# Expert stage of a one-core decoder block: 96 tokens by indirect row transfers, 160 tokens by dense plain float32 products

## What is computed

```python
q = (hf @ wq).reshape(T, PEER_HEADS, 2, PEER_DQ // 2)
s = jnp.einsum('thcd,hckd->thck', q, subkeys)
v_top, i_top = lax.top_k(s, PEER_TOPK)
...
ids = jnp.take_along_axis(cand_i, best_pos, axis=-1)
g = jax.nn.softmax(best_s, axis=-1)
...
ub = jnp.take(u_tab, idb, axis=0)
act = jax.nn.gelu(jnp.einsum('tkd,td->tk', ub, xb))
vb = jnp.take(v_tab, idb, axis=0)
return jnp.einsum('tk,tkd->td', (gb * act), vb)
```

## Time and profile before

| | |
|---|---|
| median of 3 runs | 2117.13 us (2108.36 to 2119.05) |
| the profiled execution's own time | 2113.12 us |
| its span in the profile | 2111.3 us |
| PE busy | 2066.6 us (98%) |
| DVE busy | 1383.3 us (66%) |
| ACT busy | 743.5 us (35%) |
| moved by DMA | 500.33 MB, 237 GB/s over the span |
| granted clock of PE | 0.993 of full speed in the mean |

### The profile page before, as it was taken

One profiled execution on the slowest core, in us unless ns is written; L12 is line 12 of the kernel. 1 busy time (PEld: TensorE's weight loads), 2 busy tenths in 40 slices (PEclk: granted clock), 3 DMA queues, 4 the chain that ended last, 5 costly groups with the idle time before them and its releaser, 6 DMA issues.

```text
span 2111.3 us, 30984 instructions
## 1 busy us (share of the span) xinstructions
PE 2066.6 (98%) x12256; PEld 1859.3 (88%) x12256; DVE 1383.3 (66%) x1840; ACT 743.5 (35%) x791; POOL 16.1 (1%) x30
## 2 busy tenths in 40 slices
PE   8999999989999999999999999999999999999998
PEld 6888888779988998999999999999999999999786
DVE  6685774968698976555555556556555555555797
ACT  2014114354212335343443443433433433433333
POOL 0000000000000000000000000000000000000100
PEclk9999999999999999999999999999999999999999
DMA  9999885864442666654655555555555546545995
GB/s 390 421 418 393 283 350 223 314 261 170 170 143 97 239 257 261 216 204 173 225 195 180 217 194 192 206 194 203 201 187 211 203 176 219 203 173 204 349 413 148
DMA packets 99208, 500.33 MB, mean 237 GB/s; under 512 B 8416, under 2 KB 41488, under 8 KB 42960
## 3 DMA queue, kind: packets, MB, share of 16 engines
q1 hardware_dynamic: 81840, 362.27, 46.5%
q10 hardware_dynamic: 13680, 112.20, 14.2%
q0 software_dynamic: 3632, 25.06, 3.0%
HBM read 477.32 MB, written 22.18 MB: 237 GB/s over the span
## 4 chain that ended last, share of the span: by engine, by line
PE 88%; DMA 7%; DVE 3%; ACT 1%; SPq 0%; issue 0%; ACTq 0%; DVEq 0%
PE ps L506 16%; PE ps L497 11%; PE ps L496 11%; PE ps L495 11%; PE ps L789 5%; DMA mod_first<-wmod 5%; PE ps L800 5%; PE ps L801 5%; PE ps L802 5%; PE ps L790 5%; PE ps L791 5%; PE ps L746 3%; PE ps L645 1%; DMA vraw<-vtab 1%; PE ps L646 1%; PE ps L647 1%
## 5 line engine op out<-in xcount | busy, mean ns | idle before, releaser
L497 PE MATMUL ps<-h_hi,wlo 128*128 128x256 f32 x1952 | 552.4, 283 | 0.0
L495 PE MATMUL ps<-h_hi,whi 128*128 128x256 f32 x1728 | 488.9, 283 | 1.6 <-DVE wlo L1533 1.6
L496 PE MATMUL ps<-h_lo,whi 128*128 128x256 f32 x1728 | 489.0, 283 | 0.0
L1571 DVE TENSOR_TENSOR yacc<-yacc,ps 128x512 f32<-128x512 f32 x208 | 142.9, 688 | 367.0 <-PE ps L802 367.0
L497 PEld LDWEIGHTS ps<-h_hi,wlo 128*128 128x128 f32 x1952 | 374.4, 192 | 0.0
L1537 DVE TENSOR_TENSOR vlo<-vraw,vhi 128x2048 fp32r<-128x2048 f32 x116 | 260.8, 2288 | 127.4 <-ACT vhi L1123 127.4
L495 PEld LDWEIGHTS ps<-h_hi,whi 128*128 128x128 f32 x1728 | 331.5, 192 | 3.8 <-DVE wlo L1533 1.8
L496 PEld LDWEIGHTS ps<-h_lo,whi 128*128 128x128 f32 x1728 | 331.5, 192 | 2.0
L1099 ACT ACTIVATE whi<-wraw 128x2048 fp32r<-128x2048 f32 x120 | 229.3, 1915 | 149.6 <-DMA wraw<-wst 144.2
L1533 DVE TENSOR_TENSOR wlo<-wraw,whi 128x2048 fp32r<-128x2048 f32 x120 | 269.5, 2285 | 16.4 <-ACT whi L1099 16.3
L1077 ACT ACTIVATE act_u<-ps 128x256 f32 (+1 forms) x128 | 49.1, 384 | 632.8 <-PE ps L497 569.9
(11 more groups left out here) (269 smaller groups left out, 2667.6 us busy)
## 6 DMA issues: line engine op xcount, KB each, us to landing
vraw<-vtab SPq DMA_DIRECT2D x116, 1024.0 KB, 6.8
wraw<-wst SPq DMA_DIRECT2D x111, 1024.0 KB, 4.9
wraw<-wst ACTq DMA_DIRECT2D x91, 1024.0 KB, 6.7
mod_ring<-wmod SPq DMA_DIRECT2D x58, 1024.0 KB, 10.9
mod_first<-wmod SPq DMA_DIRECT2D x22, 1024.0 KB, 20.0
gates_dram<-gstage ACTq DMA_DIRECT2D x4, 4096.0 KB, 17.0
gring<-gates_dram SPq DMA_DIRECT2D x64, 256.0 KB, 5.1
g_ring<-wmod POOLq DMA_DIRECT2D x16, 1024.0 KB, 9.2
```

The source lines that it names most:

```text
L495: mm(dst, hi, src_hi, start=first, stop=False)
L496: mm(dst, hi, src_lo, start=False, stop=False)
L497: return mm(dst, lo, src_hi, start=False, stop=last)
```

## The change

Tokens 0 to 95 (`N1`) get their picked rows, the other 160 (`N0`) stay dense.

*The 96 tokens.* DVE makes row numbers (`gidx`) of the first half's picks, PE turns h back to token rows (`hrow`). For each of the 128 picks GpSimd issues an indirect transfer that brings one row of `utab` for each of 96 tokens into a partition of its own (`gat`, 768 KB), and DVE multiplies and sums it with `hrow` (`dot`). After GeLU and gate (`row_weights`), 128 more transfers bring rows of `vtab`, and DVE adds each, times its weight, to `yacc` (`add_row`). There are two buffers `gat` for the first 30 dots and three after that.

*The 160 tokens.* U blocks and V blocks are plain products; nothing is rounded. The gates go straight from PSUM to `p0` in SBUF, with no way through DRAM, and are multiplied there in batches of 8 blocks (`weights`). V starts when all U blocks are done. The tile of V is the stationary operand and the 160 weights move, so y comes out turned; 6 banks of PSUM hold it over all 128 blocks. V is read in its stored order: `vnat[:, m, :]` takes for each partition a row of 8 KB, 1 MB after that of the partition before. `y_rows` turns y back with the last gain on the diagonal (`diag_g2`). The tiles of that gain are loaded from ACT's queue, each summed after six `add_row`.

The core of the diff:

```diff
-G2_RING = 3
-GB = 2
+G2_RING = 2
+N1 = 96
+N0 = T - N1
+PICKS = PEER_H * TOPK
 EARLY = 20
-LAG = 24
+HELD = 48
+BATCH = 8
+V_RING = 8
+LAST_V = 4
...
+            with sp.Fori(0, (NB - W_RING) // W_RING) as i:
+                for j in range(W_RING):
+                    n = N_U + W_RING + j
+                    sp.wait_ge(s_wmm, i * W_RING + (n - W_RING + 1))
+                    load_w(n % W_RING, i * W_RING + n)
+
+            for m in range(NB):
+                if m < W_RING:
+                    sp.wait_ge(s_wmm, N_U + NB - W_RING + m + 1)
+                elif m < V_RING:
+                    sp.wait_ge(s_p0, NB // BATCH)
+                else:
+                    sp.wait_ge(s_vmm, m - V_RING + 1)
+                sp.dma_start(v_slot(m), vnat[:, m, :]).then_inc(s_v[m % V_RING], 16)
...
+            def u_chunk(j, n, i, k):
+                chunk(j, n, i, k, src=h32, low=N1)
...
+            def v_tile(m, kk):
+
+                return mm(ps_y[kk], v_slot(m)[:, kk * P:(kk + 1) * P], p0[:, m, :], start=(m == 0 and kk % 3 == 0),
+                          stop=(m == NB - 1), skip_group_check=True)
...
+            def dot(k):
+
+                slot, count, _ = gather_slot(k)
+                if k == 0:
+                    dve.wait_ge(s_hrow, 4)
+                dve.wait_ge(s_gat[slot], count)
+                V.scalar_tensor_tensor(gat[slot][0:N1], gat[slot][0:N1], 1.0, hrow[0:N1], ALU.mult, ALU.mult,
+                                       accum_out=dots[0:N1, k:k + 1]).then_inc(s_used, 1)
...
+            for k in range(PICKS):
+                add_row(k)
+                if k % 6 == 5 and k // 6 < KD:
+                    add_g2(k // 6)
+                if k == 6 * KD:
                     part_done(5, M_G2)
-
+                    dve.wait_ge(s_modv, 4)
+                    dve.wait_ge(s_vmm, p0_free(141.5))
+                    V.tensor_tensor(diag_g2[:], ident.unsqueeze(1).to_broadcast([P, KD, P]),
+                                    modv[:, 5, :].unsqueeze(2).to_broadcast([P, KD, P]), ALU.mult).then_inc(s_dg2, 1)
+                    V.memset(ysb[:, :, 0:N1], 0.0).then_inc(s_yzero, 1)
...
+            pool.wait_ge(s_wmm, N_U)
+            pool.wait_ge(s_gidx, 1)
+            for g in range(2 * PICKS):
+                slot, _, held = gather_slot(g)
+                if g == S0_DOTS + 2:
+                    pool.wait_ge(s_gmm, SPREADS)
+                elif held is not None:
+                    pool.wait_ge(s_used, held + 1)
+                k = g % PICKS
+                pool.indirect_dma_start(out=gat[slot][0:N1], out_offset=None, in_=utab if g < PICKS else vtab,
+                                        in_offset=bass.IndirectOffsetOnAxis(ap=gidx[0:N1, k:k + 1], axis=0)).then_inc(s_gat[slot], 16)
```

More of the change, by code:

```diff
@@ L747, in spread @@
                 r.then_inc(s_gmm, 1)
[L749 to L750 removed]
+            for b in range(EARLY, HELD):
+                lo, hi = spreads_of(b)
                 def between(kk):
[L752 to L756 removed]
@@ L1090, in _ @@
                     act.wait_ge(s_gx, tt + 1)
                     A(pick_t[:, tt, 2], pick_t[:, tt, 2], ACT.Exp).then_inc(s_ge, 1)
-            for tt in range(TT):
-                act.wait_ge(s_pkt, tt + 1)
-                A(picks[:, :, tt * P:(tt + 1) * P], ps_spread[tt][:, 0:3], ACT.Copy).then_inc(s_pkr, 1)
-            def w_hi(j, n, i, k):
-                act.wait_ge(s_w[j], turns(i, k, W_RING) * 16)
-                A(whi[:, j], wraw[:, j], ACT.Copy).then_inc(s_whi, 1)
-            per = SPREADS // (EARLY - FIRST)
@@ new lines, in weights @@
+            def weights(i):
+                dve.wait_ge(s_wev, N_U + (i + 1) * BATCH)
+                blocks, held = slice(i * BATCH, (i + 1) * BATCH), i * BATCH % HELD
+                V.tensor_tensor(p0[:, blocks, :], act_u[:, held:held + BATCH, :], p0[:, blocks, :], ALU.mult).then_inc(s_p0, 1)
+            done = 0
+            for n in range(SPREADS):
+                one_hots(n)
+                while done < (n + 1) * S0_DOTS // SPREADS:
+                    dot(done)
+                    done += 1
@@ new lines, in _ @@
+            dve.wait_ge(s_gev, SPREADS)
+            for i in range(NB // BATCH):
+                if i < HELD // BATCH:
+                    until = S0_DOTS + 2 * (i + 1)
+                else:
+                    n0, steps = S0_DOTS + 2 * (HELD // BATCH), (NB - HELD) // BATCH
+                    until = n0 + (PICKS - n0) * (i - HELD // BATCH + 1) // steps
+                if i < HELD // BATCH:
+                    weights(i)
+                while done < until:
+                    dot(done)
+                    done += 1
+                if i >= HELD // BATCH:
+                    weights(i)
```

643 lines of the change are left out of this document (240 added, 403 removed).

## The result

The changed kernel takes **2405.04 us** (median of 4 runs, 2401.44 to 2415.77) against 2112.74 us of the kernel before (median of 4 runs, 2106.7 to 2119.05). The ratio is 1.139, with a 95% interval of 1.134 to 1.145: slower by 14%. The forecast was 1955, the range ended at 2110. The profiled execution took 2406.44 us with a span of 2404.6.

The account below looks back on a forecast made before the run. PE bounds the old kernel; after the change DMA at 400 GB/s was to decide U. Stages ending at 660, 820, 1222, 1809 and 1931, plus 20 us of end, gave span 1951, forecast 1955 against 2117; 8-in-10 range 1830 to 2110.

Parts of the forecast that it names:

- the price of a gather: GpSimd's queue: 96 rows of 8 KB, 0.786 MB at 200 GB/s, take 3.93 us in a ring of three buffers.
- PE's floor: Whole kernel: PE's work alone, with 20 us of end, would need a span of 1736 us.
- Picks to 660: 568.7 to 660 us: PE's 3.1 us wait for DVE goes, as PE has 91 us of work instead of 82.
- Spreading to 820: Gate spreading from 660: 30 dots over two gather buffers take 117 to 168 us, taken as 160, against PE's 157.
- U to 1222: Rest of U from 820: DMA decides, 161.0 MB at 400 GB/s in 402 us, against PE's 346.
- V to 1809 and 1931: V stage: 427 us shared with 96 gathers, 37 blocks at PE's pace to 1809, last 31 rows 122 us to 1931.
- The wait for block 103: At the 97th row DVE stops until V block 103 is done, holding later adds and gathers: 1809 against 1757 us.
- DMA at its best: Rival, chance 0.12: DMA engines move 419 GB/s and V's queue gets what it asks for; 1850 us.
- V slow by its pitch: Rival, chance 0.13: V loads with rows 1 MB apart cost 3.3 to 3.9 us instead of 2.6; 2005 to 2045.
- Gathers with a pace of their own: Rival, chance 0.25: each gather takes g whatever the bandwidth, time 880 + 225g; 2023 at 5.08 us, no faster from 5.47.
- the wait of a gather behind a DVE instruction: GpSimd's gathers blocked by DVE's two SBUF inputs: at most one dot, 3.3 us a gather, under 3.93, changing nothing alone.
- DVE always waiting with DMA shares under 0.8: Profile sign of a wrong forecast: it would mean the gathers' own pace rules.

Follow-up runs that it names:

- the probe: The changed kernel with 128-row gathers, plus stages of plain 8 KB-row loads after its last store: 96 partitions alone 3.3 us a load, 128 alone 2.49 us.
- the last probe: The changed kernel with 128-row gathers, plus eleven stages of GpSimd loads after its last store; indirect ones took 3.08 us for 96 rows, 2.49 us for 128.
- the kernel with 128 rows: The changed kernel with 128 rows in each gather instead of 96, the extra 32 unused: 2009.06 us, ratio to the kernel before 0.949.

## Why the prediction was wrong

**The step that failed** is the price of a gather: "0.786 MB at 200 GB/s is 3.93 us", out of 400 GB/s in all. It scaled the price of a 128-partition load to 96 partitions by bytes. In every row of before that gave 380 to 419 GB/s the loads were of 128 partitions; none had another count. Measured: 3.3 us alone where the bytes at 419 GB/s give 1.9, and 272 GB/s in all beside SP's loads. That the range's ends for the rate, 380 and 419, came from one shape made it too narrow by far.

**The size of it.** From 849 to 2381 us (1532 us) SP's queue moved 215.0 MB, 205 blocks, GpSimd's 226 gathers, and ACT's 22 MB. At the prices of the probe: 205 x 2.49 = 510, 226 x 3.3 = 746, 22 MB 52 us; 1308, times the 1.10 of the mix 1440; plus 26 us of idle DMA engines in the stretch without gathers: 1466 of 1532, within 5%. With the 3.08 us of an indirect load in the last probe it would be 1410, 8% short, so the sum rests on a price known to a tenth. With 2.49 for a gather the same sum is 510 + 563 + 52 = 1125 us; the kernel with 128 rows took 1155 from the end of its spreading (830) to its last row (1985).

**Step by step.**
- *What bounds the kernel before, the plain product's price, PE's floor:* right. 0.136 us a record (four V blocks, 128 records, start 17.38 us apart without gathers), and a span of 1736 us without gathers, as forecast.
- *Picks to 660:* right; the gates' products begin at 658 and PE's wait there is gone.
- *Spreading to 820:* until 849. The form was right (two buffers, one dot, one issue, one landing for each), the landing longer than the 4.8 to 8.3 us assumed: a gather issued at 704.6 is used at 717.4, the next, from 712.0, at 724.2, 12 to 13 us after the start of their issue. By the probes it is the same mis-sized term; with 128 rows the stage ended at 830.
- *U to 1222:* until 1448. That the DMA engines decide was right, and with 128 rows the stage ends at 1222 with 419 GB/s; the change itself has 272.
- *V to 1809 and 1931:* block 103 was done at 2223 and the last row added at 2382. Nearly equal bytes for both queues were right in form (62.9 MB for SP's, 59.5 for GpSimd's, 13.2 for ACT's, from 1500 to 2000 us), but that is 126 and 119 GB/s, not 200.
- *The wait for block 103:* there, 129 us. Its removal gained nothing, where the forecast had priced it at 52 us: without it the stretch at PE's pace comes at the end instead.
- *End:* 22 us, forecast 20.

**The rivals.** *DMA at its best* had the right rate for 128-partition loads (421). *V slow by its pitch* is refuted here: 421 GB/s in the V stage with 128-row gathers beside, and no wait of PE without gathers. The rule on the row pitch in the Trainium skill (DMA: Bandwidth & Descriptors, Latency and other measured facts) is for copies between tensors in HBM; in these loads into SBUF, with rows of 8 KB 1 MB apart, no loss shows. *Gathers with a pace of their own* had the right sign and nearly the right pace (5.85 us), by a wrong mechanism: it wanted GpSimd or the round trip to be slow, whatever the bandwidth; GpSimd needs 0.91 us, and with the blocks at their full pace beside it, the formula gives 880 + 225 x 5.85 = 2196. The measured 2405 is more, because slow gathers take DMA time away from everyone.

**A sum to set right.** For the wait of a gather behind a DVE instruction the prediction took 3.3 us a gather, with a landing of 4.8 us, which is that of one queue alone. With its own 8.3 us for two full queues it is (2.37 + 2.3 + 0.53 + 8.3)/3 = 4.5 us, over the 3.93, so by its own rows that wait would not have been harmless. The issues measured 1.06 and 1.18 us in the mean, so nothing came of it.

**The sign in the profile.** The prediction named "DVE always waiting with DMA shares under 0.8" as the mark of a wrong forecast. What came was DVE waiting with shares of 1.01. The case missing was a full engine at a low rate. And one sign of being right, a DMA share over 0.9 from 820 on, came true with the forecast 450 us off: a share tells nothing without its GB/s. The page of the Trainium skill that was weighed for DVE's port holds, in another section (SBUF — State Buffer, Door 1: The DMA port swizzle), the rule on partitions, which wasn't weighed. It would not have saved the forecast: by its map 0 to 95 reach all 16 ports, and by the fullest port a gather of 96 costs what one of 128 does, an estimate. The forecast would have been near the 2009 us of the kernel with 128 rows: still the wrong side.

## What to carry to other kernels

Price a transfer by its shape, not its bytes: when a change brings a load with another number or place of partitions than any row shows, no GB/s of the old trace bounds it, and a small probe behind the last store settles it. Try loads over all 128 partitions even where some rows are waste; here 33% more bytes in each gather saved 396 us. Read DMA share and GB/s together: here a share near 1 at two thirds of the known rate meant dear transfers, and a share of 0.8 at the same rate meant that nobody asked for more.
